# The neighbourhood bias by a skewed copy in DRAM and a mask on GpSimd, in place of Toeplitz matmuls and VectorE additions

## The reference

```python
row_off = key_rows - r[:, None] + NA_ROWS - 1
col_off = clip(c[None, :] - c[:, None], -(NA_COLS - 1), NA_COLS - 1) + NA_COLS - 1
bias = rpb[:, row_off[:, None, :, None], col_off[None, :, None, :]]
s = where(in_win[:, None, :], s + bias[None], -inf)      # in_win: 16 columns around the query
```

## Time and profile before

| | |
|---|---|
| median of 3 runs | 1180.08 us (1178.98 to 1180.6) |
| profiled execution, from first to last instruction | 1179.9 us, some 0.2 us below the median |
| PE busy | 1053.5 us, 89% |
| PE weight loads busy | 1002.2 us, 85% |
| DVE busy | 769.8 us, 65% |
| ACT busy | 552.4 us, 47% |
| POOL busy | 306.6 us, 26% |
| DMA | 131.96 MB, mean 112 GB/s |
| mean granted TensorE clock | 0.949 of 2.4 GHz |

### The profile page before, as it was taken

How to read it: one execution, slowest core, us unless ns; L and a number is a source line. 1 busy time by engine, 2 the same in 40 slices (tenths; PEclk the granted TensorE clock), 3 DMA queues, 4 the chain that set the end, 5 groups by cost and what they waited for, 6 DMA issues and landing times.

```text
span 1179.9 us, 22353 instructions
## 1 busy us (share of the span) xinstructions
PE 1053.5 (89%) x8474; PEld 1002.2 (85%) x8474; DVE 769.8 (65%) x1289; ACT 552.4 (47%) x1048; POOL 306.6 (26%) x280
## 2 busy tenths in 40 slices
PE   3889779989999998999868897899999999989987
PEld 3889779989889898889858897799998888988987
DVE  3976964665468766565558869556654677764763
ACT  3775434444325554444357654345432346554442
POOL 1462510543420002311024523125504100131110
PEclk9989989999989998999978898899999899989999
DMA  6543323323214334446344353233241242434553
GB/s 172 162 126 109 108 72 99 90 64 108 73 46 134 108 108 129 122 129 201 100 128 146 106 143 96 68 89 108 65 116 37 72 143 81 134 114 129 153 177 109
DMA packets 136023, 131.96 MB, mean 112 GB/s; under 512 B 14172, under 2 KB 134244, under 8 KB 135780
## 3 DMA queue, kind: packets, MB, share of 16 engines
q1 hardware_dynamic: 128454, 129.40, 37.8%
q10 hardware_dynamic: 7454, 1.05, 0.5%
HBM read 127.27 MB, written 3.15 MB: 111 GB/s over the span
## 4 chain that ended last, share of the span: by engine, by line
PE 34%; DVE 8%; ACT 3%; issue 2%; POOL 2%; DMA 1%; ACTq 1%; SPq 0%; POOLq 0%; DVEq 0%
PE pj L599 6%; PE pj L601 6%; PE pj L600 6%; PE mb L722 5%; DVE w_low L1315 2%; PE mb L599 1%; PE mb L593 1%; PE mb L600 1%; PE mb L601 1%; ACT w_high L1007 1%; DMA ring<-in_w_in 1%; DVE big L1390 1%; PE mb L782 1%; PE mb L918 0%; PE mb L868 0%
## 5 line engine op out<-in xcount | busy, mean ns | idle before, releaser
L1315 DVE TENSOR_TENSOR w_low<-ring,w_high 128x512 fp32r<-128x512 f32 x464 | 349.1, 776 | 225.7 <-ACT w_high L1007 224.1
L1007 ACT ACTIVATE w_high<-ring 128x512 fp32r<-128x512 f32 x464 | 287.1, 630 | 328.4 <-PE pj L601 245.4
L599 PE MATMUL pj<-w_high,h_high 128*128 128x256 f32 x1184 | 352.7, 298 | 27.7 <-DVE w_low L1315 27.7
L600 PE MATMUL pj<-w_low,h_high 128*128 128x256 f32 x1184 | 342.8, 289 | 0.0
L601 PE MATMUL pj<-w_high,h_low 128*128 128x256 f32 x1184 | 342.4, 289 | 0.0
L599 PEld LDWEIGHTS pj<-w_high,h_high 128*128 128x128 f32 x1184 | 235.9, 199 | 33.2 <-issue 31.8
L600 PEld LDWEIGHTS pj<-w_low,h_high 128*128 128x128 f32 x1184 | 235.9, 199 | 2.0 <-issue 1.9
L601 PEld LDWEIGHTS pj<-w_high,h_low 128*128 128x128 f32 x1184 | 235.0, 198 | 0.0
L1012 ACT ACTIVATE big<-mb 128x512 f32<-128x512 f32 (+2 forms) x188 | 99.5, 559 | 114.0 <-PE mb L722 52.2
L722 PE MATMUL mb<-big 128*128 128x128 f32 x1024 | 135.6, 289 | 14.2 <-POOL big L1823 12.6
L722 PEld LDWEIGHTS mb<-big 128*128 128x128 f32 x1024 | 128.9, 204 | 19.1 <-POOL big L1823 14.2
(11 more groups left out here) (256 smaller groups left out, 1789.5 us busy)
## 6 DMA issues: line engine op xcount, KB each, us to landing
ring<-in_w_in SPq DMA_DIRECT2D x368, 256.0 KB, 2.9
ring<-in_w_branch SPq DMA_DIRECT2D x64, 256.0 KB, 3.0
ring<-in_w_out SPq DMA_DIRECT2D x32, 256.0 KB, 2.9
out_x<-btm SPq DMA_DIRECT2D x12, 256.0 KB, 3.8
btm<-out_x SPq DMA_DIRECT2D x8, 256.0 KB, 4.9
tab<-in_table SPq DMA_DIRECT2D x1, 1340.0 KB, 9.3
btm<-in_x SPq DMA_DIRECT2D x4, 256.0 KB, 4.6
mid<-in_w_in ACTq DMA_DIRECT2D x4, 64.0 KB, 4.4
```

What stands on the lines that cost most here:

```text
L599: mm(o, r32(a), r32(b), start=start, stop=False, skip_group_check=True)
L600: mm(o, r32(a), r32(b_low), start=False, stop=False, skip_group_check=True)
L1007: f(r32(w_high[:, u % PARTS]), ring[:, u % RAW], ACT.Copy).then_inc(w_rounded, 1)
L1315: tt(r32(w_low[:, u % PARTS]), ring[:, u % RAW], w_high[:, u % PARTS], ALU.subtract).then_inc(w_split, 1)
```

## The change

The constants `toeplitz` and `pick`, the load of rpb, the matmul L620, ACT's copy L1095 and all b_bias steps on PE and DVE go. In their place:

- SP, after the first unit of the blocks 3 to 10 of each layer, issues `spread_rpb(h)` for one head: DRAM to DRAM, 7 row offsets x 64 copies x 128 floats (448 rows of 512 bytes, 229 KB) into the new DRAM tensor `skew`.
- SP, after each of the units 112 to 127, issues `load_bias(i)`: 64 partitions x 8 heads x 64 floats (512 runs of 256 bytes, 128 KB) of `skew` into `bias`. The partition pitch in DRAM is 127 floats where a row has 128, which gives the skew. The first waits for all spreads and for ("w", 3). Eight of them make tile 0, eight tile 1.
- POOL, in a new step b_window after a_sum, waits for the eight loads of a tile and adds the window mask to 128x2048 elements in place, one instruction for each tile. It stands on POOL between the rstd of a_sum and the diagonals of d_rows.
- b_score on DVE waits for b_window.

```diff
@@ order
-    add(("uw", 2), ("scan_v", 2), ("uw", 3), ("b_bias", 0), ("b_bias", 1), ("scan_o", 2), 1, ("b_bias", 2), ("scan_v", 3), ("b_bias", 3),
-        ("scan_o", 3), ("a_sum",), ("b_bias", 4), 1, ("a_gate", 0), ("a_gate", 1), ("b_bias", 5), 1, ("a_out", 0), ("a_out", 1), 2,
-        ("b_bias", 6), ("b_bias", 7))
+    add(("uw", 2), ("scan_v", 2), ("uw", 3), ("scan_o", 2), 1, ("scan_v", 3),
+        ("scan_o", 3), ("a_sum",), 1, ("b_window",), ("a_gate", 0), ("a_gate", 1), 1, ("a_out", 0), ("a_out", 1), 2)
...
+        skew = nc.dram_tensor("skew", (NAH, 7, C, P), F32).ap()
...
@@ SP
+                    def load_bias(i):
+                        t, half, slot = i // (2 * STEPS), i // STEPS % 2, i % STEPS
+                        row = (CHUNKS[0] + CHUNKS[1])[slot] - CHUNKS[t][half]
+                        if i == 0:
+                            sp.wait_ge(rpb_spread, 16 * NAH)
+                            sp.wait_ge(*filled(("w", STEPS - 1)))
+                        src = bass.AP(skew.tensor, (row + 3) * C * P + GRID - 1, [[P - 1, C], [7 * C * P, NAH], [1, C]])
+                        sp.dma_start(bias[rows_of(half), t, :, slot * C:(slot + 1) * C], src).then_inc(bias_in[t], 16)
+                    def spread_rpb(h):
+                        table = na_rpb[layer, h]
+                        first = table.offset + 4 * RPB_C + WIN - 1 - (GRID - 1)
+                        src = bass.AP(table.tensor, first, [[RPB_C, 7], [0, C], [1, P]])
+                        sp.dma_start(skew[h], src).then_inc(rpb_spread, 16)
...
                         load_unit(unit)
+                        if unit % UN == 0 and UN * 3 <= unit < UN * (3 + NAH):
+                            spread_rpb(unit // UN - 3)
+                        after = unit - (UN * block_no[("o", 1)] + RAW)
+                        if 0 <= after < 2 * NT * STEPS:
+                            load_bias(after)
@@ ACT
-                    act.dma_start(rpb[0:NAH * RPB_R, :], na_rpb[layer].rearrange("h r c -> (h r) c")).then_inc(params_in, 16)
@@ DVE
                             n = group_no(t, q)
+                            dve.wait_ge(windowed, t + 1)
@@ POOL
+                    def b_window():
+                        for t in range(NT):
+                            pool.wait_ge(bias_in[t], 16 * 2 * STEPS)
+                            v = bias[:, t].rearrange("p h (k c) -> p (h k) c", k=STEPS)
+                            pool.tensor_tensor(v, v, over(K("window"), NAH * STEPS), ALU.add).then_inc(windowed, 1)
```

More of the change, by code:

```diff
@@ L103, in constants @@
     out["window"] = np.tile(np.where(win, 0.0, -BIG), (2, 1))
[L105 to L112, removed]
     return {k: np.asarray(v, np.float32) for k, v in out.items()}
@@ L476, in build @@
         gained_b = sem("gained_b")
+        bias_in = [sem(f"bias_in{t}") for t in range(NT)]
+        rpb_spread = sem("rpb_spread")
+        windowed = sem("windowed")
         b_max = sem("b_max")
@@ L617, in gatecols @@
                         pe.wait_ge(params_in, 16 * PARAMS)
-                        pe.wait_ge(*room(mb[5], "rpb"))
-                        m = NAH * RPB_R
-                        mm(mb[5].t[0:RPB_C, 0:NAH * 7], rpb[0:m, :], K("pick")[0:m, :], start=True, stop=True).then_inc(mb[5].full, 1)
                         pe.wait_ge(small_split, 3)
@@ L827, in c_mix @@
                         last.then_inc(mb[4].full, 1)
[L829 to L837, removed]
                     def b_turn_in():
@@ L958, in _ @@
                         b_out=lambda t: y_turn("b", t, mb[5], 1), d_out=lambda t: y_turn("d", t, mb[4], 3),
-                        c_qkt=c_qkt, c_score=c_score, c_turn=c_turn, c_mix=c_mix, b_bias=b_bias, b_turn_in=b_turn_in, b_score=b_score,
+                        c_qkt=c_qkt, c_score=c_score, c_turn=c_turn, c_mix=c_mix, b_turn_in=b_turn_in, b_score=b_score,
                         b_turn=b_turn, b_mix=b_mix, d_prep=d_prep, d_rows=d_rows, d_turn=d_turn, d_scan=d_scan, branch=branch, merge_turn=merged_turn)
@@ L1093, in gatecols @@
                         take("small", small_T[0:32], lambda b: b[0:32, 0:S])
-                        act.wait_ge(*filled("rpb"))
-                        f(rpbT[0:RPB_C], mb[5].t[0:RPB_C, 0:NAH * 7], ACT.Copy).then_inc(mb[5].free, 1)
                     def gatecols_turn():
@@ L1585, in b_sum @@
                         gate_y("b", t, 0.5)
-                    def b_bias(i):
-                        if i == 0:
-                            dve.wait_ge(*filled(("w", STEPS - 1)))
-                        dve.wait_ge(*filled(("bias", i)))
-                        b = bank_of(("bias", i))
-                        src = b.t[0:C, 0:8 * 56].rearrange("p (c h o) -> p h o c", c=8, h=NAH)
-                        for t in range(NT):
-                            for half in range(2):
-                                r = CHUNKS[t][half]
-                                dst = bias[rows_of(half), t].rearrange("p h (k c) -> p h k c", k=STEPS)[:, :, :, 8 * i:8 * i + 8]
-                                win = K("window")[0:C, 8 * i:8 * i + 8][:, None, None, :].to_broadcast([C, NAH, 2, 8])
-                                tt(dst[:, :, 0:2], src[:, :, 3 - r:7 - r:3], win, ALU.add)
-                                last = tt(dst[:, :, 2:4], src[:, :, 4 - r:6 - r], win, ALU.add)
-                        last.then_inc(b.free, 1)
                     def b_square():
@@ L1731, in _ @@
                         scan_o=scan_o, a_sum=a_sum, a_gate=a_gate, d_gate=d_gate, proj=proj, c_prep=c_prep, c_rotate=c_rotate, c_score=c_score, c_mix=c_mix,
[L1732 removed]
+                        c_sum=c_sum, b_sum=b_sum, b_square=b_square, b_prep=b_prep, b_score=b_score, b_mix=b_mix, d_prep=d_prep,
                         d_rows=d_rows, d_m=d_m, d_step=d_step, d_scan=d_scan, d_den=d_den, d_sum=d_sum, branch=branch)
@@ L1918, in _ @@
                     run(norm=norm, rope=make_rope, conv=conv, cols=cols_diagonals, a_norm=a_norm, rows=rows, solve0=solve0, t1=t1, uw=uw, scan_o=scan_o,
-                        a_sum=lambda: sum_rms("a"), d_sum=lambda: sum_rms("d"), c_prep=c_prep, b_prep=b_prep,
+                        a_sum=lambda: sum_rms("a"), d_sum=lambda: sum_rms("d"), c_prep=c_prep, b_prep=b_prep, b_window=b_window,
                         d_prep=d_prep, d_rows=d_rows, d_m=d_m, d_step=d_step, d_scan=d_scan, branch=branch)
```

5 lines of the change are left out of this document (1 added, 4 removed).

## The result

The changed kernel takes 1192.73 us (median of 4 runs, 1190.65 to 1197.55), the kernel before beside it on the same chip 1180.34 (1178.98 to 1182.14). The ratio is 1.011, 95% interval 1.008 to 1.014: slower by 12 us, where 17 us faster was predicted. The profiled execution has a span of 1189.2 us against 1179.9.

A forecast was written before the change was run, and what follows sets the result against it. PE, busy 89% of the span, was taken as the bound. 1179.9 - 18.1 (PE) - 1.2 (ACT's queue) + 0.5 (DMA) + 2.0 (POOL) = 1163.1, plus 0.2 to the median: 1163 us, range 1152 to 1176.

The forecast's parts named there:

- Added on the DMA engines: Spreads and bias loads delaying weight loads: 0.5 us booked for all of it, bounds 0 and 25 us.
- rival D: Spreads, queued ahead of three of their block's four loads, delay PE by 1.6 us each: 1189 us, chance 0.09.
- the 3.9 us of slack: Blocks from 50 to 100 us: at least 8.3 us a block less 4.4 us landing; a longer spread delays PE.
- Added on POOL: Window additions of 4.2 us, two a layer, holding DVE splits: 0.5 us each, 2.0 us in all, bounds 0 and 17.
- about a block: PE uses a DVE split about a block (5.95 us) later, of which ACT and DVE need 1.5 to 3 us.
- rival C: Bias load 15 is late, d_rows' diagonals come 4.7 us late and PE idles there: 9.4 us, 1173 us, chance 0.20.
- Removed from PE: The b_bias matmuls go, 9.06 us a layer: 18.1 us gained, bounds 16.0 to 18.5.
- rival E: Waits that now end with b_bias end no earlier, PE idles where it worked, nothing is gained: 1179 us, chance 0.04.
- The idle time before scan_o(3): PE's wait for DVE's L1463 stays about 1.15 us; 2.2 would show 1.06 us of b_bias(3) lost.
- DVE's relief: 128 adds, some 35 us over both layers, leave DVE; none booked as gain, only cover for what POOL does to DVE.
- ACT's queue: The rpb load's issue at the start of each layer goes, 0.64 us a layer: 1.2 us booked, bounds 0 and 1.3.
- Rival B: PE's low clock near scan_o(3) to block 28 goes too, 3.3 us more a layer: 1157 us, chance 0.20.

The follow-up runs named there:

- e9: The changed kernel with each spread reading 448 different 512-byte rows of the weights, at one distance, so the bias has other numbers: 1167.97 us, ratio 0.9888.
- e16: e9 with the seven groups of 64 rows at an irregular distance, so that the outermost size stays 7: 1168.17 us, ratio 0.9895.
- e7: The changed kernel with the same spreads issued on ScalarE's queue, behind the same blocks' first weight split, instead of SyncE's: 1172.40 us, ratio 0.9920.
- e2: The changed kernel with the spreads issued at blocks 16 to 23 in place of 3 to 10: 1169.79 us, ratio 0.9902.
- e3: e2 with each tile's window addition over 128x64 instead of 128x2048, the mask left out: 1156.24 us, ratio 0.9785.
- e6: e2 with two bias loads behind each of eight weight loads instead of one behind each of sixteen: 1174.07 us.
- e10: The changed kernel with one DMA at block 3 copying the whole 14.9 KB table 64 times, in place of eight spreads: 1173.61 us, ratio 0.9925.
- e13: e10 with the second window addition behind the d_rows diagonals, both additions cut into four, and the table copy at block 16: 1165.72 us, ratio 0.9879.

## Why the prediction was wrong

**The step that failed is "Added on the DMA engines".** It booked 0.5 us; the spreads cost 23, near the end of its own bounds (25), and by the mechanism of rival D: loads behind a spread land late, the splits come late, PE idles 20.8 us in place of 10.4 from block 3 to 9. The 55.6 ns of q1, the upper price of a packet, came mostly from weight loads of 1 KB, in which no byte is read twice; a 512-byte packet from different rows takes 30 to 32 ns (e9, e16), and one of a spread 57.5 on average in after and 64 on e7's queue. The upper price was thus right by luck; the 0.5 us stood near the cheap end, 12.7 ns, because the packets are small. The sum also divided over sixteen engines: on seven, 448 packets are 3.7 us at 57.5 ns and 4.1 at 64, on both sides of the 3.9 us of slack from which D decides. I had the slack, the seven engines and the deciding point, and gave D 0.09. The rule of the Trainium skill (page "DMA: Bandwidth & Descriptors", section "Why a DMA increments its semaphore by 16 and not by 1") stood beside the sum as changing nothing, because 3.6 is under 3.9; 0.3 us between two estimates is no margin. The runs agree with the rule: sixteen engines bring 10 us. They also bound it: with fast packets seven engines cost nothing (e16).

The test itself was the wrong one. What counts is not the sum of a spread's packets but its time from issue to last packet together with what it holds up: 5.5 to 9.4 us, 7.9 on average, and weight loads landed in 8.0 us instead of 3.1, longer by 4.9 with three loads behind each spread. And 3.9 us is no slack that every block has: the 8.3 us under it are a mean, while the blocks 2 to 9 take between 6.1 and 11.3 us on PE before the change. The first new wait, the 2.10 us at 46.99, lies in block 3, right behind the shortest of them. D's cost of 26 us was close by luck: with 7.9 us a spread its own rule gives 16 x 4.0 = 64 us.

**"Added on POOL", the size of the term.** Booked 2.0 us, measured 13.6 in e2 and not measured in after itself. Two parts were off. First, DVE is held until the addition ends, so that its instructions take 4.29 and 5.53 us by the trace; that is the rule of the Trainium skill's page "SBUF — State Buffer" (section "Who interferes with whom"), to which I gave a weight of about one eighth (0.5 of 4.2). Bounds and rule were right, the value taken was not. Secondly, the cover of "about a block" was not enough even for a weight split: PE waited 0.79 to 1.17 us for it and 0.9 more for L1503 behind it, and block 29 grew by 3.0 us a layer (e2 against e3). The wait of PE for d_rows' diagonals behind the second addition is rival C's place: 1.30 us instead of its 4.7. The loads landed late (load 15 was issued at 368.64 and the addition began at 375.58), but PE's frame was late too. e6 shows that an earlier load is no cure.

**"Removed from PE", a wait that it took for none.** It said that behind the other groups PE goes straight on. Behind b_bias(6) and (7) PE had a wait of 0.34 us in b_turn_in, which Rows 3 don't show; in e3 it is 1.94 and 1.30 us. So 1.6 and 1.0 us of the 2.00 that each pair took are lost again, which is rival E in small.

**What held.** Matmuls of 6.00 us a layer go between block 27 and 29, and 8.1 and 9.7 us are gained there; the part above 6.00 fits the clock (below). 260 matmul records are gone: the 256 of the forecast and the four of L620. The idle time before scan_o(3) is 1.28 us (1.15 booked), so b_bias(3) was no filler of a wait. No run shows what DVE's relief brought. ACT's queue: block 2 of layer 1 is 1.0 us earlier, but layer 2 gains nothing there (+7.0 at the end of layer 1, +7.1 at its block 2); 1.2 us were booked.

**Rival B came too, in part in layer 1 and in full in layer 2.** Windows of the kernel after: length, busy of PE, PEld, DVE, ACT, POOL; clock, DMA share, GB/s.
```profile
342.00:346.00 4.00, 2.72 (x32) 1.91 (x30) 1.83 (x3) 1.11 (x2) 0.00 (x0) 1.00 0.98 224
346.00:351.00 5.00, 5.00 (x30) 4.09 (x29) 1.29 (x2) 1.22 (x3) 0.00 (x0) 0.66 0.46 87
381.00:389.00 8.00, 6.84 (x25) 4.73 (x26) 7.93 (x10) 1.18 (x3) 4.91 (x5) 0.59 0.48 132
...
938.00:942.00 4.00, 3.86 (x31) 2.85 (x32) 0.00 (x0) 0.60 (x1) 0.00 (x0) 1.00 0.85 182
```
In layer 1 the clock still falls after the idle time before scan_o(3), but returns sooner. In layer 2 (scan_o(3) starts at 938.14) it doesn't fall at all, and so it is in both layers of e2 and e3. The gain above the 6.00 us of matmuls is 2.1 and 3.7 us; B said 3.3. A new stretch near the 1.2 GHz level comes after PE's idle times at b_turn_in and d_rows. The first is a gain that the forecast left out, the second a loss that comes in part with the window additions: layer 1 of e3 has it too (0.66 from 368 to 372), layer 2 of e3 has not.

**With the spreads out of the way** the forecast would have been 1163, and e2 has 1169.8: some 11.6 us more than booked for the additions and 2.6 for b_turn_in, less some 7 us that the clock gave back. e3 without both is at 1156.2, near rival B's 1157, which is partly luck: B's number has 2.5 us for spreads and additions in it and nothing for b_turn_in.

**What stays open.** Why rows read over and over are slow is not shown, only that they are, and not apart from their alignment and nearness; nor was it tried how few repetitions are harmless. Why e10's copy costs 3.0 us in layer 1 and 0.7 in layer 2 was not taken apart, nor why the clock falls near scan_o(3) in layer 1 of after and not in layer 2.

## What to carry to other kernels

Before a transfer goes ahead of loads in one queue, work out its time there with the engines that its outermost size gives it and with a packet price from a transfer like it, and compare it with the shortest block, not the mean one; where no row has a price, take a margin, or issue it where the queue has room, which gave 23 us here. A group of matmuls that goes away can have stood before a wait: look at the next wait behind it, too, however short it is. A long GpSimd instruction with operands in SBUF counts as VectorE time of the same length, as far as VectorE's instructions beside it have two inputs in SBUF (in e6 L1517 with one took its usual 0.68 us beside the second addition, L1499 with two 4.43): see what VectorE does beside it and what is queued behind it, and cut or place it so that neither feeds TensorE at once. Here the late copies alone make the new way 11.6 us faster than the kernel before (e2); with all of it e13 is 14.5 us faster than the kernel before and 27 us faster than the change as it was.

## What was not expected of the hardware

- 512-byte packets from DRAM to DRAM that read one row 64 times took 64 ns on ScalarE's queue, and 57.5 (seven engines) and 78.9 (sixteen) on average in the weights' queue; from different rows 31.5 and 29.8.
- Whether a copy goes over seven or sixteen engines can be read from the packets of its queue: 455 for each spread with seven (448 and one for each engine), 464 with sixteen.
- The same slow copies issued on another queue, and later, cost about 3 us in place of 23 (e7 against e2).
- Four GpSimd additions of 128x512 beside VectorE took 5.9 to 7.4 us, where one of 128x2048 took 4.5 to 5.1: they take turns with VectorE between instructions, not within one.
- An issue of the spread took SyncE's queue 0.80 us with an outermost size of 7 and 0.57 with 64, a weight load 0.37.
